# State-space taps on four blocks of 32 output partitions instead of two

## The reference

```python
lam_bar = jnp.exp(lam * step)
b_bar = ((lam_bar - 1.0) / lam)[:, :, None] * b_mat
bu = jnp.einsum('bsgc,gnc->bsgn', u.astype(jnp.complex64), b_bar)
_, states = lax.associative_scan(_ssm_combine, (a, bu), reverse=reverse, axis=1)
return jnp.real(jnp.einsum('bsgn,gcn->bsgc', states, c_mat))
```

## Time and profile before

| | before |
|---|---|
| time, median of 3 runs | 3823.53 us (3823.15 to 3823.73) |
| the profiled execution's own time | 3826.7 us |
| its span | 3824.9 us |
| PE busy | 3322.8 us (87%) |
| DVE busy | 1669.0 us (44%) |
| ACT busy | 1335.2 us (35%) |
| tap matmuls (L2309) | 256 records, 135.5 to 416.6 us |
| TensorE clock granted, mean | 0.969 |

### The profile page before, as it was taken

One profiled execution on the slowest core, in us unless ns is written; L12 is line 12 of the kernel. 1 busy time (PEld: TensorE's weight loads), 2 busy tenths in 40 slices (PEclk: granted clock), 3 DMA queues, 4 the chain that ended last, 5 costly groups with the idle time before them and its releaser, 6 DMA issues.

```text
span 3824.9 us, 38365 instructions
## 1 busy us (share of the span) xinstructions
PE 3322.8 (87%) x13402; PEld 2351.3 (61%) x13402; DVE 1669.0 (44%) x2500; ACT 1335.2 (35%) x2005; POOL 2233.5 (58%) x1172
## 2 busy tenths in 40 slices
PE   6899999997688788777777779999999999889997
PEld 5788877885243234232222358887888787668775
DVE  7788435315657447545744542222222222121332
ACT  3566566444111001000100024444444444343553
POOL 5200366887544544454554448777777777665555
PEclk9899999998899999999999999999999999988998
DMA  5444444566999999999999955455545555444434
GB/s 160 124 134 124 147 145 138 182 223 237 415 417 420 422 419 420 421 422 420 422 420 422 419 218 176 160 171 165 171 160 171 165 171 163 137 162 129 129 130 141
DMA packets 238682, 936.34 MB, mean 245 GB/s; under 512 B 37664, under 2 KB 39840, under 8 KB 171680
## 3 DMA queue, kind: packets, MB, share of 16 engines
q0 software_dynamic: 73728, 536.90, 33.8%
q1 hardware_dynamic: 156576, 390.13, 31.5%
q10 hardware_dynamic: 8192, 6.90, 0.6%
HBM read 927.02 MB, written 2.10 MB: 243 GB/s over the span
## 4 chain that ended last, share of the span: by engine, by line
PE 52%; DMA 23%; POOL 10%; issue 6%; DVE 4%; ACT 3%; ACTq 1%; DVEq 1%; POOLq 0%; SPq 0%
PE products L668 29%; DMA arena<-peer_up_in,arena 18%; PE products L1279 8%; POOL weights_low L611 8%; PE products L1801 7%; DMA arena<-peer_down_in,arena 4%; POOL arena L1746 2%; DVE arena L1094 1%; PE products L1036 1%; PE products L2334 1%; PE products L2309 1%; ACT weights_high L599 1%; DVE arena L1755 1%; PE products L1059 1%; ACTq L2249 1%
## 5 line engine op out<-in xcount | busy, mean ns | idle before, releaser
L611 POOL TENSOR_TENSOR weights_low<-arena,weights_high 128x1024 fp32r<-128x1024 f32 x524 | 1284.1, 2457 | 513.3 <-ACT weights_high L599 512.1
L1801 PE MATMUL products<-arena 128*128 128x512 f32 x1984 | 937.9, 618 | 316.2 <-DMA arena<-peer_up_in,arena 233.9
L599 ACT ACTIVATE weights_high<-arena 128x1024 fp32r<-128x1024 f32 x612 | 647.2, 1061 | 1103.0 <-PE products L668 1064.4
L668 PE MATMUL products<-weights_high,input_high 128*128 128x512 f32 x2432 | 994.6, 409 | 23.6 <-POOL weights_low L611 15.0
L668 PE MATMUL products<-weights_low,input_high 128*128 128x512 f32 x2432 | 956.6, 393 | 0.0
L668 PE MATMUL products<-weights_high,input_low 128*128 128x512 f32 x2432 | 954.1, 392 | 0.0
L1801 PEld LDWEIGHTS products<-arena 128*128 128x128 f32 x1984 | 369.0, 194 | 868.3 <-issue 450.1
L1755 DVE SCALAR_TENSOR_TENSOR arena<-arena 128x2048 f32<-128x2048 f32 x256 | 586.3, 2293 | 522.7 <-DMA arena<-peer_down_in,arena 522.3
L1746 POOL DMA_INDIRECT arena<-peer_up_in,arena x256 | 387.6, 1514 | 527.0 <-PE products L1801 507.6
L668 PEld LDWEIGHTS products<-weights_high,input_high 128*128 128x128 f32 x2432 | 461.5, 190 | 122.1 <-issue 22.0
L668 PEld LDWEIGHTS products<-weights_low,input_high 128*128 128x128 f32 x2432 | 460.1, 189 | 100.5
(11 more groups left out here) (318 smaller groups left out, 3007.4 us busy)
## 6 DMA issues: line engine op xcount, KB each, us to landing
arena<-dsa_in SPq DMA_DIRECT2D x320, 512.0 KB, 3.4
arena<-w_in_in SPq DMA_DIRECT2D x128, 512.0 KB, 3.8
arena<-mla_wide_in SPq DMA_DIRECT2D x97, 512.0 KB, 3.4
arena<-w_attn_o_in SPq DMA_DIRECT2D x32, 512.0 KB, 3.7
arena<-w_out_in SPq DMA_DIRECT2D x32, 512.0 KB, 3.7
arena<-peer_w_query_in SPq DMA_DIRECT2D x32, 512.0 KB, 4.5
arena<-dsa_w_out_in SPq DMA_DIRECT2D x32, 512.0 KB, 3.7
arena<-glu_w_b_in SPq DMA_DIRECT2D x16, 512.0 KB, 3.7
```

The costliest lines, as they stand in the source:

```text
L599: nc.scalar.activation(w_hi[:, u % RING, :, at], ring[:, u % RING, :, at], ACT.Copy).then_inc(hi_made, 1)
L611: ops.tensor_tensor(w_lo[:, u % RING, :, at], ring[:, u % RING, :, at], w_hi[:, u % RING, :, at].bitcast(F32), op=ALU.subtract).then_inc(l ...
L668: mm = nc.tensor.matmul(PS[:, bank(b) + t, 0:width], x[:, x0 + n, at], y, start=n == 0 and m == 0, stop=n == len(parts) * PK - 1 and m == 2)
L1801: mm = nc.tensor.matmul(PS[:, SUM_BANKS[q]], diag[:, d % ROWS], row[:, q * NC:(q + 1) * NC], start=h % 2 == 0 and n == 0, stop=bool(last))
```

## The change

The 16 tap matmuls of a group all run at step m = 1, and none at m = 2. Before, the forward direction wrote PSUM partitions 0 to 31 and the backward one 32 to 63, eight matmuls after each other on the same 32. Now the four units of a direction are halved, and the four pairs of direction and half (`tap_rows`) have a block of 32 partitions each; neighbours in program order write different blocks. In PSUM and in `taps` they now stand as 128 partitions x 256 instead of 64 x 512, so ACT's copy reads that. The layout into `TW` needs a transfer for each half, direction and place in the chunk: 16 a group instead of 8, each of half the size. Semaphore counts follow.

```diff
-        taps = cols.take(4, SSM_COLS)
+        taps = cols.take(2, SSM_COLS)
...
+        def tap_rows(d, h):
+
+            two = 2 * SSM_C
+            return slice(two * (2 * d + h), two * (2 * d + h + 1))
...
-                sp.dma_start(TW[at, 0, :, i * two:], taps[0:two, :, 0:(CHUNK - i) * two]).then_inc(taps_in, 16)
-                sp.dma_start(TW[at, 1, :, 0:(i + 1) * two], taps[two:2 * two, :, (CHUNK - 1 - i) * two:]).then_inc(taps_in, 16)
+                for h in range(2):
+                    q = slice(2 * h, 2 * h + 2)
+                    sp.dma_start(TW[at, 0, q, i * two:], taps[tap_rows(0, h), :, 0:(CHUNK - i) * two]).then_inc(taps_in, 16)
+                    sp.dma_start(TW[at, 1, q, 0:(i + 1) * two], taps[tap_rows(1, h), :, (CHUNK - 1 - i) * two:])\
+                        .then_inc(taps_in, 16)
...
             if m == 2 and k >= 0:
-                act.wait_ge(taps_made, 2 * k + 2)
-                wait_from(act, taps_in, 16 * 2 * CHUNK * k)
-                nc.scalar.activation(taps[0:4 * SSM_C].rearrange("p q n -> p (q n)"), PS[0:4 * SSM_C, TAP_BANK],
+                act.wait_ge(taps_made, k + 1)
+                wait_from(act, taps_in, 16 * 4 * CHUNK * k)
+                nc.scalar.activation(taps.rearrange("p q n -> p (q n)"), PS[:, TAP_BANK, 0:2 * SSM_COLS],
                                      ACT.Copy).then_inc(taps_read, 1)
...
-            if m in (1, 2) and k >= 0:
-                d = m - 1
+            if m == 1 and k >= 0:
                 pe.wait_ge(c_spread, 2 * k + 2)
                 wait_from(pe, taps_read, k)
-                for q in range(4):
-                    u = 4 * d + q
+                for q in range(2):
                     for r in range(2):
-                        plain = BP[:, u, r, 0 if d else CHUNK - 1].rearrange("p w c -> p (w c)")
-                        mm = nc.tensor.matmul(PS[2 * SSM_C * d:2 * SSM_C * (d + 1), TAP_BANK, q * SSM_COLS:(q + 1) * SSM_COLS], plain,
-                                              CP[:, u, r, d:d + CHUNK].rearrange("p m w c -> p (m w c)"),
-                                              start=r == 0, stop=r == 1)
+                        for d in range(2):
+                            for h in range(2):
+                                u = 4 * d + 2 * h + q
+                                plain = BP[:, u, r, 0 if d else CHUNK - 1].rearrange("p w c -> p (w c)")
+                                mm = nc.tensor.matmul(PS[tap_rows(d, h), TAP_BANK, q * SSM_COLS:(q + 1) * SSM_COLS], plain,
+                                                      CP[:, u, r, d:d + CHUNK].rearrange("p m w c -> p (m w c)"),
+                                                      start=r == 0, stop=r == 1)
                 mm.then_inc(taps_made, 1)
```

More of the change, by code:

```diff
@@ L2066, in spread_b @@
             act.wait_ge(zeroed, 1)
-            wait_from(act, taps_made, 2 * k)
+            wait_from(act, taps_made, k)
             src = flat_mix[:, B_SUM[ri]:B_SUM[ri] + n].rearrange("p (x u c) -> p u x c", x=CHUNK, u=UNITS)
@@ L2321, in ssm_pe @@
             if m == 6 and k >= 0:
-                pe.wait_ge(taps_in, 16 * 2 * CHUNK * (k + 1))
+                pe.wait_ge(taps_in, 16 * 4 * CHUNK * (k + 1))
                 pe.wait_ge(state_ready, k + 1)
```

## The result

The changed kernel took 3856.51 us (median of 4 runs, 3851.56 to 3859.91) against 3823.34 us before: 33 us or 0.9% slower, ratio 1.0089 (95% interval 1.0073 to 1.0104). The forecast was slower, 3844 us; the time lies above the range of 3824 to 3853. The profiled execution took 3855.7 us, with a span of 3853.9 us, 29.0 longer than that of before.

The account below looks back on a forecast made before the run. Each group was taken as DVE alone up to the y products, then PE alone, with the taps beside DVE. Clock falls 4 x 4.9, late fills 2.2, less 1.5, gave +20.3 on 3823.5: 3844 us, range 3824 to 3853.

Parts of the forecast that it names:

- DVE's leg: Each group from m = 0 to the y products: DVE works alone, taps lie beside it, PE arrives just when DVE is done.
- item 6: PE idle 1.8 to 2 us before y drops the clock in 4 of seven groups, 4.9 us each; k = 0 already paid.
- rival A: The forecast: blocks overlap, PE idles before y, clock falls in some groups; two falls 3835 us, six 3851; chance 0.54.
- item 3: PE's 2.0 us at the y products: gain 0 for k = 1 to 6, 1.5 us once in k = 7.
- item 2: Tap matmuls: partial overlap, 32 records in about 1.8 us, PE gains about 2.0 us a group.
- The lower bound of 0.9 us: Time of the 32 tap records if four blocks run fully beside each other, which would save 2.9 us.
- rival B: Tap blocks don't overlap, PE idles only 0.5 us before y: +5.6, 3829 us; chance 0.21.
- C: Tap blocks overlap but the clock holds: 3823.5 + 3 = 3826 us; chance 0.11.
- D: DVE's path follows ACT and PE, all 2.06 us pass in each of eight groups: 3810 us, faster; chance 0.06.
- E: Changing the block costs some 0.1 us at 15 places, taps take 5 us: +12 + 4, 3839 us; chance 0.08.
- Term 4: Eight more SP transfers a group make the m = 4 fill late: 2.2 us in k = 3 and 5, half kept.

Follow-up runs that it names:

- experiment 1: Changed kernel with six more matmuls of 256 columns on PE ahead of the wait for the y products: 3825.47 us, ratio 1.0012.
- experiment 5: Kernel before with its tap transfers alone cut in two, sixteen a group of half the size, matmuls as before: 3827.66 us, ratio 1.0020.
- experiment 6: Changed kernel with only eight of its sixteen tap transfers a group, y then wrong: 3859.41 us, ratio 1.0105.
- experiment 3: Kernel before with half of its tap matmuls left out, same blocks and transfers, y then wrong: 3835.84 us, ratio 1.0038.
- experiment 4: Changed kernel with tap matmuls in loop order d, h, q, r, so four in a row write the same block: 3845.31 us, ratio 1.0061.

## Why the prediction was right and where it was wrong

The direction and the mechanism stood. PE's saving reached the y products as idle time because DVE's leg had not moved (L2183 still ends 0.1 us ahead of them), and the idle time made the clock fall; experiment 1 shows it by putting work in its place, experiments 5 and 6 clear the transfers of all but some microseconds, experiment 3 makes the harm without any blocks.

The failed step is item 6 of the sum, "I take 4 of the seven groups k = 1 to 7", at "4.9 us" each: 19.6 us. There were six falls, and those of k = 1 to 5 cost 6.2 us each. The count alone would not have left the range, since rival A's own sum with six falls gives 3851 us; the price, 1.3 us more in each, did. In the terms of the sum: six falls at 6.2 are 37.2; item 3 gave back 2.2 in k = 7 instead of 1.5, if the fall at k = 6 cost 6.2 as well; the late fills added nothing that shows; and the 5.0 of k = 0 and the 1.1 ahead of it come off. That is 28.9 us between the profiled executions. I had let the fall of k = 0 stand in both ("k = 0 has paid already"), and since the profile of after had none there, the difference of the profiled executions looks 5 us smaller than it is.

Behind item 6 stands item 2, "I take the middle": the blocks overlap nearly fully, 32 records in 1.01 us and not 1.8, so PE saved 2.8 us and not 2.0 and idled 2.6 instead of "1.8 to 2". The lower bound of 0.9 us was on record and right, but the sum didn't use it, on the argument that two records of one matmul must follow each other. They do not hold back the neighbours. Over the fifteen profiled executions a longer idle time goes with more falls (the table in the last section), and mostly with longer ones: of the 23 falls behind 2.6 us or more 18 are 13.6 us long and 5 are 10.2; of the 15 behind less, 2 are 13.6 and 13 are 10.2. In the two kernels of the case and in experiments 3, 4 and 6 a group with the long one takes 44.4 to 44.7 us, one with the short one 43.0 to 43.2. That it is the length of the idle time which sets the length of the fall is not shown: all the long ones begin from 1.1 us ahead of the first y product to 0.9 us behind it, the short ones 1.3 to 2.8 us behind it.

But item 6 was low by its own idle time too. At 1.6 to 1.8 us the clock fell in 7 of 9 groups, which would be five of seven and not four. The count had been taken between two rows of another stage, on the ground that the y products keep PE less busy; the rows don't show that, as PE is busy throughout in both low stretches (10.20 of 10.20 us and 3.30 of 3.30).

On the overlap the prediction named two rules that point opposite ways. The Trainium skill, "TensorE: Matmul & The Clock Gate", Part 3, says that weight loads overlap running matmuls only when the row group differs. This trace does not agree: all 32 tap records use the same 128 rows and differ in the column block alone, and both their loads and their matmuls start 0.03 us apart, though a load is 0.11 us long and a record of one block takes 0.12. The same part of that page of the Trainium skill gives 2.38 times for three column tiles; the trace points the same way, with 3.7 times for four (3.72 us in two batches, 1.01 in one).

Point by point: rival B (no overlap) is out. C (the clock holds) is what experiment 1 made, at +4.9 us where C said +3. D (DVE's leg follows PE) is out: the state was ready 22.17 us after the first tap in both. E (changing blocks costs) is out by the 1.01 us. Term 4 (late fills) is hidden in the changed kernel, where the groups that end at k = 3 and 5 take 44.7 and 44.4 us like their neighbours, since a fall makes the group longer than the fill is late; alone it was 2.6 us for 4.4 taken. In k = 7 the taps' landing bound, as said: 1.73 us of idle time named DMA; the group there cost 4.0 us net because of the fall at k = 6, and the clock kept 1.00 behind the 1.73 us.

## What to carry to other kernels

Where two engines reach a meeting point together, a saving on one is idle time on that one; count it as a gain only after naming who else must arrive and by how much they lead. If the engine is PE, the idle time isn't free: here 2.6 us of it ahead of the y products halved the clock for 13.6 us. Put work there, useful or not, or shorten the other legs first, and measure the saving again after that: the change that cost 33 us was worth 13 in the right surroundings, earlier laying of the taps included.

## What the runs showed of the hardware that was not expected

- Matmuls on four blocks of 32 output partitions in plain float32 overlap nearly fully, 1.01 us for 32 records against 3.72 us for the same in batches on one block each, and still in part when neighbours share a block (a row 2.46 us long where the changed kernel's is 1.08).
- A 2.38 us subtraction on POOL beside DVE held a DVE multiplication of 0.69 us until it was done (3.50 us for two instead of 1.30), and so three times in each of k = 1 to 6.
- How often the clock fell at the y products, by how long PE had idled just ahead of them, over all eight groups of the fifteen profiled executions:

| idle time | groups | falls |
|---|---|---|
| 0 to 0.12 us | 45 | 0 |
| 0.34 to 0.81 us | 15 | 0 |
| 1.05 to 1.47 us | 28 | 8 |
| 1.63 to 1.82 us | 9 | 7 |
| 2.61 to 3.04 us | 23 | 23 |

A fall counts here if it begins between 1.1 us ahead of the first y product and 2.9 us behind it. Between 1.05 and 1.82 us the same idle time did harm in one group and none in another; what decides there is not shown.
